# Two transformer blocks with a routed-expert layer: the matmuls of the value stage wait operand by operand

## The reference, cut to what matters

```python
def peer_ffn(h, w_q, sub_keys, u, v):             # per chunk of tokens xc
    q = (xc @ w_q).reshape(-1, PEER_HEADS, 2, half)
    s = jnp.einsum('thpd,pkd->thpk', q, sub_keys)
    ...                                           # top 16 of 128 x 128 experts, gates g = softmax
    ue = u[eid]
    ve = v[eid]
    a = jax.nn.gelu(jnp.einsum('td,thkd->thk', xc, ue))
    return jnp.einsum('thk,thkd->td', g * a, ve)
```

## Time and profile before

| | us |
|---|---|
| median of 3 runs (lowest, highest) | 3532.32 (3528.73, 3536.05) |
| the profiled execution, its time | 3530.44 |
| the profiled execution, its span | 3528.7 |
| PE busy (share of the span) | 3265.3 (93%) |
| DVE busy | 2171.8 (62%) |
| ACT busy | 1543.9 (44%) |

### The profile page before, as it was taken

How to read it: one execution, slowest core, us unless ns; L and a number is a source line. 1 busy time by engine, 2 the same in 40 slices (tenths; PEclk the granted TensorE clock), 3 DMA queues, 4 the chain that set the end, 5 groups by cost and what they waited for, 6 DMA issues and landing times.

```text
span 3528.7 us, 60815 instructions
## 1 busy us (share of the span) xinstructions
PE 3265.3 (93%) x20336; PEld 2856.0 (81%) x20336; DVE 2171.8 (62%) x4110; ACT 1543.9 (44%) x2941; POOL 469.3 (13%) x563
## 2 busy tenths in 40 slices
PE   6999999899998889999999999989896998988898
PEld 4779999877776745789998777779875998986798
DVE  6538878778884144288787788865433545534354
ACT  2123478744442133234788444454322444433343
POOL 0120035611110000100356111100000000000000
PEclk9999999999999766999999999999998999999899
DMA  7664544389994300345443898855431553543354
GB/s 277 219 203 157 172 156 136 115 322 317 313 313 144 107 30 18 131 159 172 158 136 109 312 317 311 312 182 184 148 133 60 184 183 127 184 134 104 102 184 143
DMA packets 176451, 632.32 MB, mean 179 GB/s; under 512 B 23608, under 2 KB 23616, under 8 KB 175328
## 3 DMA queue, kind: packets, MB, share of 16 engines
q1 hardware_dynamic: 134416, 491.48, 40.9%
q0 software_dynamic: 41920, 139.60, 11.4%
q10 hardware_dynamic: 16, 0.01, 0.0%
HBM read 627.74 MB, written 9.50 MB: 181 GB/s over the span
## 4 chain that ended last, share of the span: by engine, by line
PE 86%; DVE 7%; ACT 2%; DVEq 2%; issue 1%; POOL 1%; DMA 1%; ACTq 0%; SPq 0%; POOLq 0%
PE ps L531 20%; PE ps L411 15%; PE ps L421 10%; PE ps L423 10%; PE ps L422 10%; PE ps L519 2%; PE ps L517 2%; PE ps L518 2%; PE ps L433 2%; PE ps L464 2%; PE ps L442 2%; PE ps L788 1%; PE ps L789 1%; PE ps L494 1%; DVE unit_low L1203 1%
## 5 line engine op out<-in xcount | busy, mean ns | idle before, releaser
L1203 DVE TENSOR_TENSOR unit_low<-ring,unit_high 128x1024 fp32r<-128x1024 f32 x744 | 948.6, 1275 | 446.9 <-ACT unit_high L868 436.4
L868 ACT CAST unit_high<-ring 128x1024 fp32r<-128x1024 f32 x744 | 778.1, 1046 | 678.6 <-PE ps L423 522.6
L421 PE MATMUL ps<-expert_x_high,unit_high 128*128 128x256 f32 x1792 | 517.1, 289 | 17.6 <-DVE unit_low L1203 17.4
L422 PE MATMUL ps<-expert_x_low,unit_high 128*128 128x256 f32 x1792 | 505.0, 282 | 0.0
L423 PE MATMUL ps<-expert_x_high,unit_low 128*128 128x256 f32 x1792 | 503.6, 281 | 0.0
L411 PE MATMUL ps<-hT,ring 128*128 128x256 f32 (+1 forms) x1776 | 414.6, 393 | 49.9 <-ACT hT L903 27.2
L411 PEld LDWEIGHTS ps<-hT,ring 128*128 128x128 f32 (+1 forms) x1776 | 341.7, 195 | 114.6 <-issue 49.2
L421 PE MATMUL ps<-norm_parts,unit_high 128*128 128x256 f32 x1408 | 403.2, 286 | 27.4 <-DVE norm_parts L1208 27.4
L423 PE MATMUL ps<-norm_parts,unit_low 128*128 128x256 f32 x1408 | 401.5, 285 | 0.0
L422 PE MATMUL ps<-norm_parts,unit_high 128*128 128x256 f32 x1408 | 400.5, 284 | 0.0
L421 PEld LDWEIGHTS ps<-expert_x_high,unit_high 128*128 128x128 f32 x1792 | 342.6, 191 | 25.6 <-DVE unit_low L1203 12.4
(11 more groups left out here) (219 smaller groups left out, 5210.1 us busy)
## 6 DMA issues: line engine op xcount, KB each, us to landing
ring<-stream SPq DMA_DIRECT2D x914, 512.0 KB, 3.3
score<-ada POOLq DMA_DIRECT2D x224, 512.0 KB, 5.2
arena<-bias_tiles POOLq DMA_DIRECT2D x48, 192.0 KB, 2.7
arena<-ada SPq DMA_DIRECT2D x8, 1024.0 KB, 17.2
bias_tiles<-bias_rows POOLq DMA_DIRECT2D x8, 768.0 KB, 16.7
x_home<-x POOLq DMA_DIRECT2D x2, 1024.0 KB, 4.1
hT<-cond POOLq DMA_DIRECT2D x2, 1024.0 KB, 6.0
x<-x_home POOLq DMA_DIRECT2D x2, 1024.0 KB, 7.9
```

The costliest lines, as they stand in the source:

```text
L421: pe.matmul(out, hi[:, kt, :], xh[:, kt, :], start=(kt == 0), stop=False)
L422: pe.matmul(out, hi[:, kt, :], xl[:, kt, :], start=False, stop=False)
L868: nc.scalar.copy(hi, ring[:, unit % SLOTS, :]).then_inc(whi_ready, 1)
L1203: V.tensor_tensor(out=lo, in0=ring[:, unit % SLOTS, :], in1=hi, op=ALU.subtract).then_inc(wlo_ready, 1)
```

## The change

`spread_t` no longer waits for `wlo_ready` at its head. It waits there for the two casts, `whi_ready` and `ahi_ready`. The wait for `wlo_ready` now stands ahead of the third matmul of the unit (the first that reads the rest of the weights), and a new wait for `alo_ready` ahead of the fifth (the first that reads the rest of the activations). The wait for `alo_ready` at the head of the stage is gone. ACT, DVE, POOL and SP run the same instructions as before.

```diff
                 hi, lo = parts_of(unit, n)
-                pe.wait_ge(wlo_ready, it * per + (n + 1))
+                pe.wait_ge(whi_ready, it * per + (n + 1))
+                pe.wait_ge(ahi_ready, it * per + (a + 1))
                 for tt in range(TT):
                     toks = slice(tt * P, (tt + 1) * P)
                     for c, (act_part, w) in enumerate(((ahi, hi), (ahi, lo), (alo, hi))):
+                        if tt == 0 and c == 1:
+                            pe.wait_ge(wlo_ready, it * per + (n + 1))
+                        if tt == 0 and c == 2:
+                            pe.wait_ge(alo_ready, it * per + (a + 1))
                         for b in range(2):
...
                 a = NE * l
-                pe.wait_ge(alo_ready, a + 2)
                 for k in range(4):
                     spread_t(u + k, n + k, a + k, 0, 0, k == 0, False)
```

## The result

With the change the kernel takes 3501.54 us (median of 6 runs, 3494.62 to 3508.15); the kernel before, run beside it, 3533.32 (median of 6, 3527.56 to 3536.15). The ratio is 0.9911 (95% interval 0.9895 to 0.9927): 31.8 us faster. The profiled execution took 3503.63, its span is 3501.9, 26.8 less than before.

The account below looks back on a forecast made before the run. A circle of waits among PE, ACT and DVE was taken as the limit; 34.7 + 2.5 - 1 - 3.3 = 32.9 us gained, forecast 3498 us, range 3492 to 3515.

Parts of the forecast that it names:

- The ring: Value stages: ACT waits for PE, PE for DVE, DVE for ACT; this circle, no single engine, sets 2.93 us a unit.
- 5.87: Length in us of the circle of waits before the change, covering two units; 0.465 less with the wait at the third matmul.
- The term of 34.7: Both value stages: us gained when 240 units go from the old pace to PE's own 2.79 us.
- The slack: Steady units: PE's 5.58 us for two units exceeds the shortened circle's 5.41, leaving 0.17 us to spare.
- The dense stretch: Units 6 to 29 of a stage, with two 512 KB pieces a unit; DMA share would have to reach 1.00.
- the taking-off of 3.3: Half of the 6.7 us gain in units 6 to 29 of both stages, deducted as lost to transfers.
- The first rival, dense stretch unmoved: Two transfers a unit keep the pace in units 6 to 29: 3.3 us more, 3501 to 3503; chance 0.22.
- DVE's additions and the loads: Small additions after eight reductions, 24 times 0.17 us, may hold PE: 1 us deducted; loads were expected in time.
- the second rival: Late transfers throughout: ring loads set about 2.86 us a unit, 20 us gained, 3510 to 3512; chance 0.12.
- The start of a stage: First head 0.80 us earlier, needing only the first cast, and fifth unit's head 0.465: 2.5 us for both stages.
- Waits in the middle of a unit: Waits at the third and fifth matmul cost nothing when met; upper end 0.115 us each if they bind.
- The slower rival: Mid-unit waits hold back weight loads even when met, 2 x 0.115 us a unit: 3552 to 3554; chance 0.09.

Follow-up runs that it names:

- e4: The changed kernel with the wait for the rest of the weights one matmul earlier, at the unit's second matmul: 3509.3 us, ratio 0.9934 to the kernel before.
- e2: The changed kernel with each unit's twelve matmuls reordered, so the rest of the weights is awaited at the ninth: 3499.34 us, ratio 0.9907 to the kernel before.
- e8: The changed kernel, unedited, profiled a second time: 3502.47 us in one execution, mix1 353.9.
- e7: The kernel before, unedited, profiled a second time: 3530.25 us in one execution, mix1 349.4.
- e1: The changed kernel with only the moved wait for the rest of the weights; the activations' waits stay as before: 3503.48 us, ratio 0.9918 to the kernel before.
- e3: The changed kernel with three more already met waits in each unit's second half, 768 in all: 3501.8 us, ratio 0.9922 to the kernel before.
- shifted kernels: Kernels with extra transposes at each value stage's end, so that mix1 starts later: e9, e10 and e12.
- e5: The kernel before with weights cast and their rest made ahead of the activations', whose rest is awaited at the fifth matmul: 3505.76 us, ratio 0.992.
- e9: The changed kernel with 32 more transposes at the end of each value stage: 3501.9 us in one execution, mix1 346.2.
- e6: The kernel before with DVE's later reductions of the conditioning weights over one column instead of 1024: 3551.59 us, ratio 1.0059.
- e10: The kernel before with 32 more transposes at the end of each value stage: 3546.37 us in one execution, mix1 356.8.
- e12: The kernel before with 80 more transposes at the end of each value stage: 3549.65 us in one execution, mix1 348.2.

## Why the prediction was right, and which terms were off

**The ring: right.** 5.87 less 0.465 below 2 x 2.79 said that PE would set the pace. The pace is 2.786, and e4 puts a point between the two ends, where the same sum gives 2.82 (measured 2.81). The term of 34.7 with all that was to be taken off it in the same stretch, 34.7 - 1 - 3.3 = 30.4, came out at 32.3.

The slack was larger than the sum's 0.17. In the first stage the rest of the weights ended 0.34 ahead of the third matmul in most units (901.80 + 1.23 = 903.03, against 903.37), in none less than 0.25, and PE needs some 0.05 behind a rest that it waits for (903.08 to 903.13). So about 0.29 was to spare. Worked out from the rows, the 5.87 still holds the 0.115 by which a head's pair is longer behind a wait that binds; once it no longer binds, the ring loses that too, and 0.17 + 0.115 is 0.285.

**The dense stretch: the taking-off of 3.3 was wrong, it is 0.** I took half of a gain for lost because no row showed a share of 1.00. The rows now show 0.99 and 0.97, and 260 matmuls in 60 us in both stages. The first rival, dense stretch unmoved, is out. The Trainium skill's page "DMA: Bandwidth & Descriptors", section "Where 436 GB/s comes from", from which that rival would have followed, puts the limit at about 358 GB/s for a core; the trace shows 369 and 360 in these stretches on the one core that runs. The measurement decides: it was no limit here.

**DVE's additions and the loads: 1 taken off, about 3 measured, all in the second stage.** By the starts of the units' heads, six units of the second stage are 0.26 to 0.40 longer than 2.79, 1.8 together. Each stands behind an addition, as in the rows of DVE and PE at the first of them:

```profile
2059.77 1.22 DVE L1322 CUSTOM_DVE_ANT_0 score<-score,hT 128x1024 f32<-128x1024 f32 x1
...
2061.32 0.17 DVE L1328 TENSOR_TENSOR mods<-small,prm 128x8 f32 x1 [0.33 <-issue]
...
2061.90 1.22 DVE L1207 TENSOR_TENSOR unit_low<-ring,unit_high 128x1024 fp32r<-128x1024 f32 x1
```

```profile
2063.18 0.73 PE L536 MATMUL ps<-unit_low,expert_high 128*128 128x512 f32 x2
```

I priced the addition at its own 0.17. Here it also has 0.33 of idle ahead of it, put down to issue, and DVE has not waited since the unit before. The rest of the weights ends at 2063.12 and the third matmul starts at once behind it, 0.66 behind its head instead of 0.465. Only these six of the 24 additions have that idle time (0.31 to 0.33); the other 18, all of the first stage's among them, have 0.10 at most, and no unit behind them is longer. The kernel before has the same six, with the same idle time and units of 3.13 to 3.37 us, so the change did not bring them; in e2 the idle time is there too and no unit behind it is longer, since the rest is wanted later. Why it is these six stays open. Two more units, near 2280, are 1.2 longer together; there ACT waited 1.32 and 1.35 us for the ring's load. That was the second rival in small: transfers are late at one place, not throughout.

**The start of a stage: 2.5 expected, 1.4 measured, and not for the reason given.** PE started 0.72 earlier behind the one-hots (0.80 expected). But in the first stage nothing of it was left at the second unit's head, since the first unit's pairs ran at a granted clock of 0.50, most of them 0.85 apart; in the second stage 0.47 was left there. From the one-hots to the ninth head the two stages gained 0.77 and 0.60 (28.27 and 29.02, against 29.04 and 29.62 before; 0.39 and 0.93 in e8 against e7), and e1, which starts as late as before, gained as much. What was won came from the waits of the next units, such as that of 0.69 in the earlier trace rows.

**Waits in the middle of a unit: right at nothing.** The slower rival wanted 0.115 for each of 512 waits; e3 shows none for 768 more. The page "TensorE: Matmul & The Clock Gate" of the Trainium skill, section "Step-by-step: what each phase is for", has weight loads pulled ahead of running matmuls; the load at 903.15, ahead of its matmul at 903.37 and behind a met wait, agrees.

**mix1: not in the sum.** In the profiled execution 7.6 of the 33.8 us went to a lower granted clock in a phase that the change doesn't touch, so that the span is only 26.8 shorter. The shifted kernels show that it need not be the waits' doing. In the kernels that are built on the change (the change, e1 to e5, e8, e9) mix1 lasted 346.2 to 357.0 us; with the old order of PE's waits (before, e6, e7, e10, e12) 348.2 to 356.8. But unshifted, the change had 357.0 and 353.9 and before 349.4 twice, so a part of it may be what the medians lost: 31.8 gained, where the phases of the two stages gave 33.8. What makes the clock fall at one place of mix1 and not at another stays open.

The forecast of 3498 is 3.5 below the median. On the profiled execution: 32.9 were forecast, peer0 and peer1 gave 33.8, mix1 took 7.6, and the other phases gave the remaining 0.6. That the terms come so close to the forecast in those two phases (32.3 from the windows and 1.4 at the starts) is luck in part: 3.3 that was not lost stands against some 2 more for additions and loads and 1.1 less at the starts.

## What to carry to other kernels

Where engines wait in a circle, add up the durations from a unit's release to the instruction that really needs the last operand; moving a wait from the head to that instruction shortens the circle by the work that lies between, until another engine's own work is longer, and what is left over says what comes next (here DVE, whose rest has some 0.3 us to spare). A wait that is met cost nothing here, so operands can be awaited one by one. Compare two profiles phase by phase before naming a cause: mix1, which the change doesn't touch, moved by up to 11 us between executions, along with the granted clock.

## What the runs showed of the hardware that was not expected

- One core moved 369 GB/s for 60 us with its DMA engines at a share of 0.99, and the loads came in time.
- Less work on DVE made the kernel before 21 us slower (e6); its ring loads, issued closer to the other loads, landed in 6.3 us instead of 5.2.
- The same matmuls of mix1 took 3.72 to 6.76 us for 16, behind equal idle times, with the granted clock of the 48 us around them at 0.79 to 0.95; they differ between executions of one program and between kernels whose phase starts 5 to 6 us apart.
- Starting PE 0.7 us earlier behind idle time did not last: in the first stage the second unit came no earlier behind the matmuls ahead of the gap (7.37 us, before 7.31), in the second 0.47 earlier (7.41, before 7.88), and by the ninth unit e1, without the earlier start, was as far.
- One short addition on DVE had 0.09 us of idle ahead of it in 18 places and 0.31 to 0.33 in six, the same six in every kernel looked at (before, the change, e2).
